# Three of four squared MLP blocks turned by VectorE in 32x32 squares and placed through DRAM by SyncE's queue

## What is computed

```
u = _rmsnorm(h, norm_mlp_g[layer])
a = jnp.einsum('bsd,df->bsf', u, w_up[layer])      # 2048 -> 8192
a = jnp.square(jax.nn.relu(a))
h = h + jnp.einsum('bsf,fd->bsd', a, w_down[layer])  # 8192 -> 2048
```

## Time and profile before

| | |
|---|---|
| median of the runs | 2288.86 us |
| span of the profiled execution, first to last instruction | 2285.8 us |
| lying around the span, against the median | 3.1 us |
| TensorE busy (PE) | 2266.4 us, 99% |
| VectorE busy (DVE) | 1556.3 us, 68% |
| ScalarE busy (ACT) | 1109.7 us, 49% |
| GpSimd busy (POOL) | 223.5 us, 10% |
| DMA | 528.12 MB, mean 231 GB/s |

### The profile page before, as it was taken

One profiled execution on the slowest core, in us unless ns is written; L12 is line 12 of the kernel. 1 busy time (PEld: TensorE's weight loads), 2 busy tenths in 40 slices (PEclk: granted clock), 3 DMA queues, 4 the chain that ended last, 5 costly groups with the idle time before them and its releaser, 6 DMA issues.

```text
span 2285.8 us, 28964 instructions
## 1 busy us (share of the span) xinstructions
PE 2266.4 (99%) x10345; PEld 1864.5 (82%) x10345; DVE 1556.3 (68%) x1869; ACT 1109.7 (49%) x1531; POOL 223.5 (10%) x361
## 2 busy tenths in 40 slices
PE   9999999999999999999999999999999999999998
PEld 7888888888888888888878877787888888888886
DVE  7886778778867877887767664556555545555556
ACT  6446455555545545545463463545444344444444
POOL 0121001111111111110011000000210011100110
PEclk9999999999999999999999999999999999999999
DMA  8983679978888888886677664564665666656663
GB/s 311 331 272 97 206 235 320 317 267 293 275 281 287 273 301 269 272 280 215 220 242 245 209 203 129 186 220 158 210 203 194 207 207 198 207 185 201 195 195 126
DMA packets 250005, 528.12 MB, mean 231 GB/s; under 512 B 22144, under 2 KB 22544, under 8 KB 248592
## 3 DMA queue, kind: packets, MB, share of 16 engines
q1 hardware_dynamic: 214256, 405.32, 54.2%
q0 software_dynamic: 33664, 116.17, 14.8%
q10 hardware_dynamic: 1952, 4.85, 0.6%
HBM read 517.87 MB, written 4.21 MB: 228 GB/s over the span
## 4 chain that ended last, share of the span: by engine, by line
PE 97%; DVE 1%; ACT 1%; DMA 0%; issue 0%; SPq 0%; ACTq 0%; DVEq 0%; POOLq 0%
PE acc L1798 30%; PE acc L1807 29%; PE acc L1802 29%; PE tp L1869 2%; PE m L1880 1%; PE acc L1820 0%; PE acc L1825 0%; PE acc L1830 0%; PE tp L2206 0%; PE tp L2224 0%; PE tp L2218 0%; PE acc L2000 0%; PE tp L2131 0%; PE acc L1853 0%; PE acc L1851 0%
## 5 line engine op out<-in xcount | busy, mean ns | idle before, releaser
L1090 DVE TENSOR_TENSOR wlo<-wring,whi 128x1024 fp32r<-128x1024 f32 x762 | 919.5, 1216 | 562.6 <-ACT whi L565 455.4
L565 ACT ACTIVATE whi<-wring 128x1024 fp32r<-128x1024 f32 (+1 forms) x510 | 532.1, 1047 | 720.4 <-PE acc L1807 719.3
L1798 PE MATMUL acc<-whi,xhi 128*128 128x512 f32 x2056 | 558.5, 393 | 0.1
L1802 PE MATMUL acc<-whi,xlo 128*128 128x512 f32 x2056 | 550.0, 389 | 0.0
L1807 PE MATMUL acc<-wlo,xhi 128*128 128x512 f32 x2056 | 549.9, 389 | 0.0
L1802 PEld LDWEIGHTS acc<-whi,xlo 128*128 128x128 f32 x2056 | 386.0, 188 | 81.1
L1807 PEld LDWEIGHTS acc<-wlo,xhi 128*128 128x128 f32 x2056 | 386.0, 188 | 80.7
L1798 PEld LDWEIGHTS acc<-whi,xhi 128*128 128x128 f32 x2056 | 381.2, 188 | 86.3 <-issue 9.0
L575 ACT ACTIVATE whi<-wring 128x1024 fp32r<-128x1024 f32 x266 | 280.8, 1059 | 319.8 <-PE acc L1807 318.1
L1120 DVE SCALAR_TENSOR_TENSOR macc<-mring,csil,macc 128x512 f32<-128x512 f32 x480 | 344.0, 747 | 29.3 <-DMA mring<-w_mod 23.0
L460 POOL DMA_DIRECT2D mring<-w_mod x192 | 138.9, 724 | 1047.4 <-DVE macc L1120 998.9
(11 more groups left out here) (277 smaller groups left out, 1313.7 us busy)
## 6 DMA issues: line engine op xcount, KB each, us to landing
wring<-w_up SPq DMA_DIRECT2D x216, 512.0 KB, 4.7
wring<-w_down SPq DMA_DIRECT2D x216, 512.0 KB, 5.1
mring<-w_mod POOLq DMA_DIRECT2D x192, 512.0 KB, 5.3
wring<-w_in SPq DMA_DIRECT2D x184, 512.0 KB, 5.2
wring<-w_gate SPq DMA_DIRECT2D x88, 512.0 KB, 4.3
wring<-w_out SPq DMA_DIRECT2D x64, 512.0 KB, 4.9
tmpT<-blk POOLq DMA_DIRECT2D x128, 32.0 KB, 3.4
gbig<-ctx_in POOLq DMA_DIRECT2D x2, 1024.0 KB, 8.1
```

Of the source, the lines that this page charges most:

```text
L565: act.activation(whi[:, piece_slot(c, piece), 0:half], wring[:, g4, piece * half:(piece + 1) * half], ACT.Copy).then_inc(hi_done, 1)
L1090: dve.tensor_tensor(wlo[:, h4, 0:half], wring[:, g4, piece * half:(piece + 1) * half], whi[:, h4, 0:half].bitcast(F32), ALU.subtract).then ...
L1798: pe.matmul(acc[:, 2 * pair + t, :], hi[:, tile, t * P:(t + 1) * P], whi[:, h4, w], start=(tile == starts), stop=False)
L1802: pe.matmul(acc[:, 2 * pair + t, :], lo[:, tile, t * P:(t + 1) * P], whi[:, h4, w], start=False, stop=False)
```

## The change

Three of the four blocks of each chunk (blocks 0, 1 and 2; MLP_MOVED = 3) are no longer turned by TensorE. VectorE transposes them in 32x32 squares (`turn_relu`) in its rounds 5, 9 and 13. SyncE stores the strips to a DRAM tensor (`store_strips`, one DMA of 256 KB) and reads them back into their places (`place_strips`, four DMAs of 64 KB), at fixed points between its weight loads. ScalarE rounds them (`round_relu`) and VectorE makes the remainders (`remain_relu`) in rounds 9, 13 and 17. Block 3 is turned by TensorE as before. TensorE waits for relu_lo ahead of groups 16 and 18.

```diff
+            def store_strips():
+                sp.wait_ge(relu_turned, c.at("rs", T, T))
+                sp.dma_start(strip_rows.rearrange("i b j n -> (i b) j n"), strips).then_inc(strips_stored, 16)
+
+            def place_strips():
+                sp.wait_ge(strips_stored, c.at("rs", 16, 16))
                 for j in range(4):
+                    sp.dma_start(placed[32 * j:32 * j + 32, :, :], strip_rows[:, :, j, :].rearrange("i b n -> b i n"))\
+                        .then_inc(relu_moved, 16)
+                c.add("rs")
+            def up_block(i, j):
+                v = w_up.rearrange("(g k p) n -> g p k n", k=KG, p=P)
+                for kg in range(KT // KG):
+                    load(v[kg, :, :, bass.ds(i * D + j * NB, NB)])
+                    if j >= 2 and kg == 1:
+                        store_strips()
+                    if j >= 2 and kg == 2:
+                        place_strips()
...
+                        if n == 0 and kg == 1:
+                            store_strips()
+                        if n == 0 and kg == 2:
+                            place_strips()
...
+                if j:
+                    act.wait_ge(relu_turned, c.at("rt", T, T))
+                    c.add("rt")
                 for t in range(T):
-                    last = act.activation(blk2[:, t, :], acc[:, 2 * (j % 2) + t, :], ACT.Relu, scale=rstd[:, 1, t:t + 1])
+                    last = act.activation(blk[:, t, :], acc[:, 2 * (j % 2) + t, :], ACT.Relu, scale=rstd[:, 1, t:t + 1])
...
-                act.activation(blk[:, :, :], blk2[:, :, :], ACT.Square).then_inc(blk_ready, 1)
+                act.activation(blk[:, :, :], blk[:, :, :], ACT.Square).then_inc(blk_ready, 1)
...
+            def round_relu(tile):
+                act.wait_ge(relu_moved, c.at("rm", RELU_MOVES, RELU_MOVES))
+                for k in range(KG):
+                    act.activation(xhi[:, tile + k, :].rearrange("p (t i b) -> p t i b", t=T, i=4),
+                                   moved[:, k], ACT.Copy).then_inc(relu_hi, 1)
+                c.add("rm")
...
                     round_group(4 * j + 1)
...
-                    if 1 <= j <= 4:
-                        round_banks(xhi, 4 * (j - 1), 2)
+                    if 2 <= j <= 4:
+                        round_relu(4 * (j - 2))
+                    if j == 4:
+                        round_banks(xhi, 12, 2)
...
+            def turn_relu():
+                dve.wait_ge(blk_ready, c.at("blk", 1))
+                dve.wait_ge(relu_moved, c.at("rt", 0, RELU_MOVES))
+                for t in range(T):
+                    dve.transpose(turned[:, t], blk[:, t, :].rearrange("p (k j b) -> p k j b", k=KG, j=4)).then_inc(relu_turned, 1)
+                c.add("rt")
+            def remain_relu(tile):
+                for k in range(KG):
+                    dve.wait_ge(relu_hi, c.at("rk", 1))
+                    dve.tensor_tensor(xlo[:, tile + k, :].rearrange("p (t i b) -> p t i b", t=T, i=4), moved[:, k],
+                                      xhi[:, tile + k, :].bitcast(F32).rearrange("p (t i b) -> p t i b", t=T, i=4),
+                                      ALU.subtract).then_inc(relu_lo, 1)
...
                     if g % 4 == 1 and 1 <= j <= 4:
-                        remain_banks(xhi, xlo, 4 * (j - 1), 2)
+                        if j >= 2:
+                            remain_relu(4 * (j - 2))
+                        if j < 4:
+                            turn_relu()
+                        c.add("blk")
+                        if j == 4:
+                            remain_banks(xhi, xlo, 12, 2)
...
                     for kg in range(3):
+                        if j == 4 and kg in (0, 2):
+                            pe.wait_ge(relu_lo, c.at("rs", KG * (2 if kg == 0 else 3), KG))
                         multiply(hi, lo, (kg,), 4, pair)
...
-                        if kg == 1 and 1 <= j <= 4:
+                        if kg == 1 and j == 4:
                             pe.wait_ge(blk_ready, c.at("blk", j))
                             turn_rows(blk, 2)
```

More of the change, by code:

```diff
@@ L55 @@
 WARM = 4
-X_HI = 2 * (2 * KG - 1) + 4 * KG + 8 * MLP_CHUNKS + 2 * KG + 2 * KG + 8
+MLP_MOVED = 3
+X_HI = 2 * (2 * KG - 1) + 4 * KG + 2 * MLP_CHUNKS + 2 * KG + 2 * KG + 8
 H0 = 2
@@ L219, in two_blocks @@
         hspill = nc.dram_tensor("hspill", [T, P, D], F32).ap()
+        strip_rows = nc.dram_tensor("strip_rows", [4, 32, 4, 2 * P], F32).ap()
         piece_landed = [[sem(f"piece_landed{i}_{piece}") for piece in range(SPLIT)] for i in range(WSLOTS)]
@@ L254, in two_blocks @@
             sem(n) for n in ("squares_turned", "rows_moved", "moved_hi", "moved_lo"))
+        relu_turned, strips_stored, relu_moved, relu_hi, relu_lo = (
+            sem(n) for n in ("relu_turned", "strips_stored", "relu_moved", "relu_hi", "relu_lo"))
         out_s = sem("out_s")
@@ L366, in two_blocks @@
         BANKS = {"z": 1, "suffix": 1, "ctx_state": 1, "state": 2, "turn": 1, "out": 1, "conv": 2}
-        T_O = 8 + 8 + 8 * MLP_CHUNKS + 8 + 8 + 4 + BANKS["out"] + sum(
+        T_O = 8 + 8 + 2 * MLP_CHUNKS + 8 + 8 + 4 + BANKS["out"] + sum(
             BANKS.get(step[0], 0) for steps in BESIDE[1].values() for step in steps)
@@ L372, in two_blocks @@
         MOVES = 16 * 16
+        RELU_MOVES = 4 * 16
         block = ctx.enter_context(nc.Block())
@@ L405, in _ @@
                     block_of(w_out, i * (2 * NB) + j * NB)
-            with c.loop(sp, MLP_CHUNKS, g=32) as i:
-                for j in range(4):
-                    block_of(w_up, i * D + j * NB)
-                for n in range(4):
-                    block_of(w_down, n * NB, kg0=i * 4)
+            def store_strips():
[3 more added lines that the diff above has]
+                sp.wait_ge(strips_stored, c.at("rs", 16, 16))
+                for j in range(4):
+                    sp.dma_start(placed[32 * j:32 * j + 32, :, :], strip_rows[:, :, j, :].rearrange("i b n -> b i n"))\
[9 more added lines that the diff above has]
+                        place_strips()
+            with c.loop(sp, MLP_CHUNKS, g=32, rs=MLP_MOVED) as i:
+                for j in range(4):
+                    up_block(i, j)
+                for n in range(4):
+                    v = w_down.rearrange("(g k p) n -> g p k n", k=KG, p=P)
+                    for kg in range(KG):
+                        load(v[bass.ds(i * 4 + kg, 1), :, :, n * NB:(n + 1) * NB].rearrange("a p k n -> (a p) k n"))
+                        if n == 0 and kg == 1:
+                            store_strips()
+                        if n == 0 and kg == 2:
+                            place_strips()
             for names in (C_IN, X_IN):
@@ L866, in _ @@
             root_and_scale(2, u_g, u_g)
-            with c.loop(act, MLP_CHUNKS - 1, 1, g=32, q=8, half=4, blk=4, ha=4, ssq=4 * T, mt=5):
+            with c.loop(act, MLP_CHUNKS - 1, 1, g=32, q=2, half=4, blk=4, ha=4, ssq=4 * T, mt=5, rt=MLP_MOVED, rm=MLP_MOVED):
                 mlp_chunk()
@@ L1381, in set_gain1 @@
                 dve.wait_ge(gain_set, 2)
+            def turn_relu():
[10 more added lines that the diff above has]
+                                      ALU.subtract).then_inc(relu_lo, 1)
+                    c.add("rk")
             def mlp_chunk(i, first=False, last=False):
@@ L1419, in _ @@
             norm_scale(2, u_g, u_g)
-            with c.loop(dve, MLP_CHUNKS - 1, 1, g=32, q=8, hi=8, m=32, ma=80, mt=5, msum=5 * KG) as i:
+            with c.loop(dve, MLP_CHUNKS - 1, 1, g=32, q=2, hi=2, m=32, ma=80, mt=5, msum=5 * KG, blk=4, rt=MLP_MOVED,
+                        rk=KG * MLP_MOVED) as i:
                 mlp_chunk(i)
@@ L2093, in mlp_chunk @@
                 c.add("blk", 4)
+                c.add("rs", MLP_MOVED)
             mlp_chunk(True)
-            with c.loop(pe, MLP_CHUNKS - 1, 1, g=32, q=8, ma=80, ha=4, half=4, blk=4):
+            with c.loop(pe, MLP_CHUNKS - 1, 1, g=32, q=2, ma=80, ha=4, half=4, blk=4, rs=MLP_MOVED):
                 mlp_chunk()
```

## The result

The kernel after takes 2322.0 us (2319.6 to 2324.3, 4 runs) where the one before took 2289.2 beside it: ratio 1.014, 95% interval 1.013 to 1.016. It is slower by 33 us; 2291.0 was forecast, with a range up to 2303. The profiled execution has a span of 2322.5 us, 36.7 more than before. In all that follows two disturbed executions are left out, one of two_steps (4641 us) and one of the kernel before beside it (3605 us).

The account below looks back on a forecast made before the run. TensorE, busy 2266.4 of 2285.8 us, was taken as the bound. Turns -10.7, relu_lo wait +12.8, VectorE and SyncE's queue zero: +2.1 on the span, 2287.9; the median lies 3.1 higher: 2291.0 us, range 2284 to 2303.

Parts of the forecast that it names:

- The turns: TensorE, blocks 0 to 2 of four chunks: twelve turns of 0.89 us leave its stream, 10.7 us off, all counted.
- The wait for relu_lo: TensorE ahead of group 18 waits for block 2's remainders, 3.2 us in each of four chunks: 12.8 us added.
- rival B: TensorE's clock falls to half in the new waits, 3.4 us lost each; 2294.4 to 2304.6 us; chance 0.33.
- VectorE's surplus: VectorE's added work on moved blocks, 1.69 us each, 20 us in all, is hidden by its lead: taken as zero.
- 13.6 us of VectorE: Up to 1.7 us for two of three blocks per chunk would show if VectorE's lead were used up; range only.
- SyncE's queue: Weight loads behind the store and placing go 8.8 and 8.4 us late but still land in time: taken as zero.
- rival C: SyncE's queue brings group 19's weights 3 us late in each chunk: slower, 2303 us; chance 0.11.
- the strips' bytes: Stores and placings in the MLP stage: 12 x 0.5 MB on 179 MB, 3.5%, fits at a DMA share of 0.85.
- Rule against row: The skill's rule keeps 128x128 turns on TensorE, leaving 2288.9 us; the row prices this at 0.89 us a block.

Follow-up runs that it names:

- two_steps: The changed kernel with two moved blocks in place of three and a new table of modulation steps, SC1 reduction behind group 16: 2284.8 us, ratio 0.9986.
- turns_vec: The kernel before with twelve turns left out on TensorE and two more VectorE transposes in rounds 9, 13 and 17, no strips: 2287.9 us.
- relu_steps: The changed kernel with block 2's moved data one round earlier and a new step table (SC1 reduction behind group 16, no step in round 13): 2284.6 us.
- relu_early: The changed kernel with block 2's moved data rounded and subtracted in round 16 in place of 17: 2304.6 us, ratio 1.0059.
- three_draws: The kernel before with twelve turns left out, two more VectorE transposes in three rounds, and stores and placings of data nobody waits for: 2296.7 us.
- full: The changed kernel with block 2's data one round earlier, SyncE's store and placing later, and a new step table (SC1 reduction behind group 16): 2294.9 us.
- dma_only: The kernel before plus the changed kernel's twelve stores and 48 placings on SyncE's queue, of data nobody waits for: 2289.9 us, ratio 1.0002.

## Why the prediction was wrong

- **The turns: right.** 10.7 us forecast; left out by themselves they gave 9.3 (0.4% of 2289.5, 0.26 to 0.54%), with 1.6 us of new waits of TensorE in the stage against them.
- **The wait for relu_lo: right.** 12.8 us forecast as four times 3.2; measured 11.9 as 3.2, 2.9, 2.9 and 2.9, in the rows and the order that were named. That the clock fell behind these waits is rival B's, below; the sum had it at nothing.
- **VectorE's surplus: this step failed.** "VectorE works two groups (some 10.9 us) ahead of TensorE, so a surplus of 1.7 us in one group is hidden by that lead. I take zero". The surplus was sized rightly (a remainder of moved data 417 ns, a transpose 686). The lead was not. It is the lead of the weights, and VectorE has a second customer: the SC1 reduction behind group 15 wants the step of round 14, which VectorE ends 0.3 us ahead of TensorE. No two groups lie there. Three things drew on these 0.3 us: VectorE later by its surplus, its waits for w_mod ahead of the reduction (1.2 to 2.3 us a chunk, and none in turns_vec, which has no strips), and TensorE earlier by the three turns themselves. The last was the saving I counted in full; part of it could only become waiting. I had kept 13.6 us of VectorE for the range, but priced each surplus for itself and added no traffic and no clock. It became 18.5 us of gaps and, with the falls behind them, some 27 (four gaps, 17.1 us at half clock, 8.5 lost).
- **Rival B: its mechanism was right, and its count too low.** The clock fell behind all four waits for relu_lo (0.33 was given for it to fall at all), and for 3.41 us, not 6.7, so 1.7 us a fall. It fell at the four SC1 gaps as well, which the prediction did not see: up to 15.4 us in all, where the sum had zero. The prediction's argument against it, that a single case does not say that each such stretch ends in a fall, did not hold in this kernel. The Trainium skill (TensorE: Matmul & The Clock Gate, "HAM oscillation") has a TensorE that idles for data set back to the lower clock and paying at every such wait; at these eight gaps the trace agrees, 3.41 or 6.83 us at 0.50 each, and at the 1.8 us gaps of turns_vec it doesn't show.
- **SyncE's queue: little in effect, and later than thought.** Group 14's first piece landed 3.9 us before ScalarE took it (3.9 forecast). Group 15's, for which 1 to 3 us to spare were forecast, came late: it landed at 586.13 after 9.4 us and not 5.2, and ScalarE, which had waited for it for 2.02 us, started at 586.23. Some 0.4 us of that are lateness, since TensorE let ScalarE go at about 585.9 (by rows elsewhere, ScalarE starts 0.2 us behind TensorE's next four matmuls, here at 585.67). So the sign of rival C was there, 19.9 us of ScalarE's waits for weights, but it was not the cause of the gaps in the last three chunks, where VectorE does not wait for ScalarE ahead of the reduction; for the first chunk that is open. But the strips' bytes, which I held against the DMA engines' share only ("fits"), reached VectorE through w_mod, on a queue that the prediction did not look at. They were also mis-sized: a block is 128 x 1024 numbers of 4 bytes, so the row has 512 KB for a store and 128 KB for a placing, not the 256 and 64 KB of the text, and 12 blocks move 12.6 MB, not 6: 7% of the stage's 179 MB. For a store of this size had no row.
- **Rule against row.** The prediction cites the Trainium skill (VectorE: DVE Perf Modes, "Rules for kernel authors"), which keeps squares of 128x128 on TensorE. The changed kernel bears it out by 33 us, relu_steps does not, by 5: what decided was where VectorE's work stood. And relu_steps is faster by 0.2% only.

## What to carry to other kernels

For each engine that gets more work, look for every place where the bounding engine waits for it or would just not wait, and read the lead there, from the end of the giving row to the start of the taking one; one lead elsewhere says nothing. Charge against that lead the work added, the DMA waits that new traffic lengthens, and the time that the bounding engine itself is made earlier, all at once, because each alone may measure as free. When a gap remains, look at where the work and the point that needs it stand before shrinking the work: a new table of steps, with the reduction one group later and no step in the fullest round, was worth 20 us here (relu_early to relu_steps). Moving the reduction alone moved the gap.

## What the runs showed of the hardware

- A gap of TensorE without data cost more than its length: at or just behind each gap of 2.87 us or more in the MLP stage of the changed kernel the granted clock was 0.50 for 3.41 or 6.83 us. Shorter gaps differ: none of the four of 1.8 us in the profiled execution of turns_vec was followed by a fall; in three_draws the one of 2.39 us was, that of 2.50 was not; one of 2.17 in full was.
- The placing of a strip (a destination of 32 partitions) of 128 KB landed 6.3 us after its issue, the store of the whole block, 512 KB, 3.1, and loads of weights issued behind the placing took 9 to 14 us to land (group 15's pieces in the second chunk: 9.4 and 11.5, group 16's 12.2 and 13.7) where the same loads took 5.6 and 6.3, 5.4 and 6.1 in the kernel before.
- 12.6 MB of extra reads and writes (6.3 MB each), with nobody waiting for the data, lengthened VectorE's waits for another queue's transfers from 22.4 to 35.3 us (dma_only), at a DMA share of 0.91 for 0.85; a median transfer of that queue landed after 6.3 us and not 5.4. The kernel took 2289.9 us for 2289.5: none of it showed in the time until the lead was used up.
